# A 640-slot matmul chain of two transformer stacks: order of work changed in six stages

## The reference

```python
# first stack: four layers, kinds A, B, C, A
for i in range(4):
    xn = rms_norm(h, norm_gain[i])
    m = diff_attention | mla | rglru_block | diff_attention    # (xn) -> y @ w_out
    h = h + m
    g = sigmoid(rms_norm(h, ple_norm[i]) @ ple_w_gate[i])
    h = h + g * (p[i] @ ple_w_proj[i])
# second stack: an SSD layer, then a dilated attention layer
for layer in range(2):
    shift, scale, gate = split(silu(c) @ ada_w[layer] + ada_b[layer], 3)
    hh = x * (1.0 + scale) + shift
    y = ssd_mixer(hh) | dilated_mixer(hh, k_sh, v_sh)
    x = layer_norm(alpha * x + (1.0 + gate) * y) * ln_g[layer] + ln_b[layer]
    if layer == 0:
        k_sh, v_sh = split(x @ kv_w, 2)
```

## Time and profile before

| | |
|---|---|
| median of 3 runs | 3638.04 us (3634.32 to 3638.28) |
| the profiled execution's own time | 3631.8 us |
| its span, first to last instruction | 3630.0 us |
| mean granted TensorE clock over the span | 0.987 |
| PE busy / DVE busy / ACT busy / POOL busy | 96% / 78% / 54% / 16% |
| mean rate of the transfers | 190 GB/s |

### The profile page before, as it was taken

One profiled execution on the slowest core, in us unless ns is written; L12 is line 12 of the kernel. 1 busy time (PEld: TensorE's weight loads), 2 busy tenths in 40 slices (PEclk: granted clock), 3 DMA queues, 4 the chain that ended last, 5 costly groups with the idle time before them and its releaser, 6 DMA issues.

```text
span 3630.0 us, 68468 instructions
## 1 busy us (share of the span) xinstructions
PE 3492.7 (96%) x27986; PEld 3410.1 (94%) x27986; DVE 2836.3 (78%) x4649; ACT 1948.7 (54%) x3084; POOL 579.3 (16%) x546
## 2 busy tenths in 40 slices
PE   7999999999999999999999999999999998999997
PEld 7999999999899989999999999999999997999997
DVE  7787887677787887877877787898989866666665
ACT  6555546566547685565555456554545546434344
POOL 2111112111113011221111112231313300000000
PEclk9999999999999999999999999999999998999998
DMA  6555556434465444656555464445454443555552
GB/s 244 211 196 216 198 222 225 172 151 175 167 274 189 175 157 182 254 180 228 198 219 202 188 251 175 152 156 216 152 209 161 154 151 123 203 204 192 208 193 93
DMA packets 104904, 691.17 MB, mean 190 GB/s; under 512 B 12688, under 2 KB 21008, under 8 KB 22672
## 3 DMA queue, kind: packets, MB, share of 16 engines
q1 hardware_dynamic: 104128, 685.14, 50.9%
q0 software_dynamic: 464, 1.64, 0.1%
HBM read 676.25 MB, written 2.10 MB: 187 GB/s over the span
## 4 chain that ended last, share of the span: by engine, by line
PE 48%; DVE 15%; ACT 5%; issue 3%; POOL 1%; DMA 1%; SPq 0%; DVEq 0%; POOLq 0%; ACTq 0%
PE g L434 14%; PE g L436 14%; PE g L435 14%; DVE w_lo L1457 4%; ACT w_hi L944 2%; DMA scratch<-scratch 1%; POOL scratch L2271 1%; PE turn_bank L473 1%; DVE scratch L1987 1%; DVE con L1987 1%; DVE sq L1951 0%; DVE scratch L1958 0%; DVE sq L1950 0%; PE norm_bank L447 0%; DVE rstd L1950 0%
## 5 line engine op out<-in xcount | busy, mean ns | idle before, releaser
L1457 DVE TENSOR_TENSOR w_lo<-w_raw,w_hi 128x1024 fp32r<-128x1024 f32 x1088 | 1342.9, 1236 | 445.7 <-ACT w_hi L944 433.5
L944 ACT ACTIVATE w_hi<-w_raw 128x1024 fp32r<-128x1024 f32 x1088 | 1134.0, 1054 | 978.1 <-PE g L436 855.2
L434 PE MATMUL g<-p_hi,w_hi 128*128 128x256 f32 x4624 | 1333.0, 288 | 35.0 <-DVE w_lo L1457 23.1
L435 PE MATMUL g<-p_lo,w_hi 128*128 128x256 f32 x4624 | 1310.9, 283 | 0.0
L436 PE MATMUL g<-p_hi,w_lo 128*128 128x256 f32 x4624 | 1310.8, 283 | 0.0
L434 PE MATMUL g<-q_hi,w_hi 128*128 128x256 f32 x3472 | 1004.5, 289 | 18.4 <-DVE scratch L2164 10.5
L436 PE MATMUL g<-q_hi,w_lo 128*128 128x256 f32 x3472 | 986.3, 284 | 0.0
L435 PE MATMUL g<-q_lo,w_hi 128*128 128x256 f32 x3472 | 986.3, 284 | 0.0
L434 PEld LDWEIGHTS g<-p_hi,w_hi 128*128 128x128 f32 x4624 | 889.4, 192 | 49.5 <-DVE w_lo L1457 33.2
L435 PEld LDWEIGHTS g<-p_lo,w_hi 128*128 128x128 f32 x4624 | 889.7, 192 | 1.4
L436 PEld LDWEIGHTS g<-p_hi,w_lo 128*128 128x128 f32 x4624 | 889.2, 192 | 0.0
(11 more groups left out here) (421 smaller groups left out, 3833.1 us busy)
## 6 DMA issues: line engine op xcount, KB each, us to landing
w_raw<-in_slots SPq DMA_DIRECT2D x640, 1024.0 KB, 4.9
scratch<-scratch SPq DMA_DIRECT2D x128, 64.0 KB, 4.9
h<-in_x SPq DMA_DIRECT2D x4, 512.0 KB, 6.3
out_h<-h SPq DMA_DIRECT2D x4, 512.0 KB, 2.6
sq<-in_p POOLq DMA_DIRECT2D x4, 256.0 KB, 3.0
con<-in_consts SPq DMA_DIRECT2D x1, 832.0 KB, 10.9
scratch<-in_distance POOLq DMA_DIRECT2D x1, 576.0 KB, 5.6
vec<-in_vecs SPq DMA_DIRECT2D x1, 383.0 KB, 3.8
```

What stands on the lines that cost most here:

```text
L434: pe.matmul(g, wh, hi[:, k], start=n == 0, stop=False)
L435: pe.matmul(g, wh, lo[:, k], start=False, stop=False)
L944: act.activation(w_hi[k % SPLIT][:, cols], raw[MAIN_AT[k] % RAW][:, cols], ACT.Copy).then_inc(hi_ready, 1)
L1457: dve.tensor_tensor(w_lo[k % SPLIT][:, cols], raw[MAIN_AT[k] % RAW][:, cols], w_hi[k % SPLIT][:, cols], SUB).then_inc(lo_ready, 1)
```

## The change

- **A heads (layers 0 and 3).** The modulation's half slots move from slots 2, 3, 6, 7 to slots 1, 2, 5, 6; the column sums from slot 1 to slot 0. The loads of these slots move with them.
- **Ends of A layers.** The projection begins with banks that the scores do not use, the modulation's column sums follow, and the first two output tiles are multiplied in parts (`begin_out`, `begin_tile`, `part`): blocks of the seven finished heads between the last head's turn, mix and norm, and its own two blocks at the end.
- **End of B and C.** In B the first output tile is multiplied in parts likewise (the last pair gives its last two blocks). In C the projection waits for the split p alone, and the first output tile takes y's blocks as they come.
- **SSD.** Rows, segments, decay and weights of the first two of a group's four pieces move from the next group's steps 0 and 1 to the own group's slots 8 and 9; the other two from steps 2, 3 to 0, 1. `s_y_out` moves from steps 2 to 5 to steps 0 to 3 and waits for the gate product of its piece; norm to 5, scale to 6, `s_y_lo` to slot 7.
- **Dilated heads.** The first head begins with q0 and q1 side by side on each arriving block of q (`two_square_tiles`), then q2, the gate, and k and v (`D_FIRST`). The p blocks are made in four portions between these slots (`D_NORM_TILES`), the odd h tiles on DVE in place of ACT. Its modulation halves stand in slots 4, 5, 8, 9, and head 0's weights 0 and 1 are turned together at its end. At the layer's end the two half tiles of the first output slot are multiplied in parts, as above.
- The gates' `model_norm` uses bank bT in place of bN.

The core of the diff:

```diff
-    heads = lambda at: [at + 8 * n + m for n in range(A_HEADS) for m in (2, 6)]
+    heads = lambda at: [at + 8 * n + m for n in range(A_HEADS) for m in (1, 5)]
...
-    return out + [454 + 10 * n + m for n in range(DIL_HEADS) for m in (0, 8)]
+    return out + [454 + 10 * n + m for n in range(DIL_HEADS) for m in (0 if n else 4, 8)]
...
+D_FIRST = (0, 1, 2, 9, 3, 4, 5, 6, 7, 8)
+D_NORM_TILES = (0, 2, 6, 11, DT)
...
+        def two_square_tiles(hi, lo):
+
+            ws = [slot(), slot()]
+            pe.wait_ge(tile_taken, c.at("tile"))
+            for n in range(SLOT):
+                if n == SLOT // 2:
+                    second_half()
+                pe.wait_ge(x_lo, c.next("x"))
+                for e, w in enumerate(ws):
+                    g = G[c.bank ^ e][:, 0:SEQ]
+                    wh, wl = w_hi[w][:, n * P:(n + 1) * P], w_lo[w][:, n * P:(n + 1) * P]
+                    pe.matmul(g, wh, hi[:, n], start=n == 0, stop=False)
+                    pe.matmul(g, wh, lo[:, n], start=False, stop=False)
+                    last = pe.matmul(g, wl, hi[:, n], start=False, stop=n == SLOT - 1)
+                    if n == SLOT // 2 - 1:
+                        last.then_inc(half_used, 1)
+                    if n == SLOT - 1:
+                        last.then_inc(tile_done, 1)
+            c.next("tile", 2)
...
+        def begin_out():
+
+            w, s = slot(), c.k["slot"]
+            return w, s, begin_tile()
+
+        def begin_tile():
+
+            c.next("tile")
+            pe.wait_ge(tile_taken, c.at("tile", -2))
+            g = G[c.bank][:, 0:SEQ]
+            c.bank ^= 1
+            return g
+
+        def part(begun, hi, lo, first, last, at=0, length=SLOT):
+
+            w, s, g = begun
+            for n in range(first, last):
+                b = at + n
+                if b == SLOT // 2:
+                    pe.wait_ge(lo_ready, 2 * s)
+                wh, wl = w_hi[w][:, b * P:(b + 1) * P], w_lo[w][:, b * P:(b + 1) * P]
+                pe.matmul(g, wh, hi[:, n], start=n == 0, stop=False)
+                pe.matmul(g, wh, lo[:, n], start=False, stop=False)
+                done = pe.matmul(g, wl, hi[:, n], start=False, stop=n == length - 1)
+                if b == SLOT // 2 - 1 and length == SLOT:
+                    done.then_inc(half_used, 1)
+            if last == length:
+                done.then_inc(tile_done, 1)
...
-                if j == 1 and prev:
+                if j == 0 and prev:
                     mod_columns([acc[:]])
...
             a_head(hi, lo, False, True)
             for n in range(1, A_HEADS):
                 a_head(hi, lo, True, False)
             pe.wait_ge(p_ready, c.next("p"))
-            w = slot()
+            w, s = slot(), c.k["slot"]
+            pe.wait_ge(factor_ready, c.at("norm"))
+            proj_half(layer, 0, w, range(4), s)
+            mod_columns([acc[:]])
+            out_0 = begin_out()
+            pe.wait_ge(x_lo, c.at("x", A_HEADS - 1))
+            part(out_0, *y, 0, 4)
             pe.wait_ge(score_read, c.at("score_read"))
-            pe.wait_ge(rot_read, c.at("rot"))
-            proj_half(0, w, range(6))
+            proj_half(layer, 0, w, range(4, 8), s)
+            part(out_0, *y, 4, 10)
             a_turn_weights()
+            part(out_0, *y, 10, 14)
             a_mix()
+            out_1 = begin_out()
+            part(out_1, *y, 0, 6)
             a_norm_out()
-            pe.wait_ge(factor_ready, c.at("norm"))
-            proj_half(0, w, (6, 7))
-            c.next("x", A_HEADS)
-            mod_columns([acc[:]])
-            out_and_gates(y, x)
+            part(out_1, *y, 6, 14)
+            pe.wait_ge(x_lo, c.next("x", A_HEADS))
+            part(out_0, *y, 14, DT)
+            part(out_1, *y, 14, DT)
+            out_and_gates(layer, y, x, 2)
...
             pe.wait_ge(p_ready, c.next("p"))
-            w = slot()
+            w, s = slot(), c.k["slot"]
+            out_0 = begin_out()
+            pe.wait_ge(x_lo, c.at("x", B_PAIRS - 1))
+            part(out_0, *y, 0, 7)
             pe.wait_ge(score_read, c.at("score_read"))
-            proj_half(0, w, range(4))
+            proj_half(layer, 0, w, range(4), s)
             b_turn_weights()
-            mod_columns([acc[:]], fresh=True)
+            mod_columns([acc[:]])
+            part(out_0, *y, 7, 10)
             b_mix()
             pe.wait_ge(turn_read, c.at("turn"))
-            proj_half(0, w, range(4, 8))
-            c.next("x", B_PAIRS)
-            out_and_gates(y, x, fresh=True)
+            pe.wait_ge(factor_ready, c.at("norm"))
+            proj_half(layer, 0, w, range(4, 8), s)
+            part(out_0, *y, 10, 14)
+            pe.wait_ge(x_lo, c.next("x", B_PAIRS))
+            part(out_0, *y, 14, DT)
+            out_and_gates(layer, y, x, 1)
...
             pe.wait_ge(p_ready, c.next("p"))
-            pe.wait_ge(x_lo, c.at("x", -2))
-            proj_half(0, slot(), range(8))
-            out_and_gates(y, x)
+            w, s = slot(), c.k["slot"]
+            proj_half(layer, 0, w, range(8), s)
+            out_and_gates(layer, y, x, 0)
...
-            if 2 <= step <= 5:
-                s_out(step - 2, turned)
             if step < 4:
-                s_rows(g, step)
-            if step == 6:
+                s_out(step, turned)
+            if step < 2:
+                s_rows(g, step + 2)
+            if step == 5:
                 s_norm()
...
-                if first and n == 3:
-                    pe.wait_ge(x_lo, c.next("x", DT))
-                square_tiles(*((p_hi, p_lo) if 3 <= n <= 8 else (q_hi, q_lo)), arriving=DT if first and n == 0 else 0)
+                kind = n if prev else D_FIRST[n]
+                if not prev and n == 0:
+                    two_square_tiles(q_hi, q_lo)
+                elif prev or n > 1:
+                    square_tiles(*((p_hi, p_lo) if 3 <= kind <= 8 else (q_hi, q_lo)), arriving=DT if not prev and kind == 3 else 0)
...
+            tile_0 = begin_out()
+            pe.wait_ge(x_lo, c.at("x", DIL_HEADS - 1))
+            part(tile_0, c_hi, c_lo, 0, 4, 0, 8)
             d_turn_weights(2)
+            part(tile_0, c_hi, c_lo, 4, 7, 0, 8)
             d_turn_values(1)
-            d_turn_values(2)
             mod_columns(d_acc)
+            w, s, _ = tile_0
+            tile_1 = w, s, begin_tile()
+            part(tile_1, c_hi, c_lo, 0, 4, 8, 8)
+            d_turn_values(2, -2)
+            part(tile_1, c_hi, c_lo, 4, 7, 8, 8)
             d_mix()
             pe.wait_ge(x_lo, c.next("x", DIL_HEADS))
-            norm_project(c_hi, c_lo, 0)
+            part(tile_0, c_hi, c_lo, 7, 8, 0, 8)
+            part(tile_1, c_hi, c_lo, 7, 8, 8, 8)
+            norm_project(c_hi, c_lo, 0, 2)
...
-                if j in (2, 3, 6, 7):
-                    ada_half([acc[:]], (j - 2) % 4)
+                if j in (1, 2, 5, 6):
+                    ada_half([acc[:]], (j - 1) % 4)
...
+            p_slot()
             a_finish(jl)
-            p_slot()
...
-            if 2 <= step <= 5:
-                s_y_out(step - 2)
             if step < 4:
-                s_segments(g, step)
-            if step == 7:
+                s_y_out(g, step)
+            if step < 2:
+                s_segments(g, step + 2)
+            if step == 6:
                 s_scale_y(g)
...
+                if n > 7:
+                    s_segments(g, n - 8)
...
-        def s_y_out(m):
+        def s_y_out(g, m):
 
             dve.wait_ge(yd_done, c.next("yd"))
+            dve.wait_ge(gluon, 10 * g + 7 + m)
...
+        def d_norm_tiles(n):
+
+            for m in range(D_NORM_TILES[n], D_NORM_TILES[n + 1]):
+                dve.wait_ge(x_hi, c.next("x"))
+                if m % 2:
+                    link(dve.tensor_scalar(h[:, m], h[:, m], V("ln_g", m), V("ln_b", m), MUL, ADD))
+                dve.tensor_tensor(p_lo[:, m], h[:, m], p_hi[:, m], SUB).then_inc(x_lo, 1)
...
+                if n in ((0, 1, 8, 9) if prev else (4, 5, 8, 9)):
                     ada_half(d_acc, n % 2)
...
```

244 lines of the change are left out of this document (137 added, 107 removed).

## The result

| | before | after |
|---|---|---|
| median | 3637.52 us (3634.32 to 3638.28, 4 runs) | 3607.58 us (3605.91 to 3611.83, 4 runs) |
| ratio after/before | | 0.9918, 95% interval 0.9905 to 0.9932 |
| span of the profiled execution | 3630.0 us | 3604.5 us |
| mean granted TensorE clock | 0.987 | 0.994 |

The change saves 25.5 us between the two profiled executions and 30 us between the medians. The forecast was 3594 us with a range of 3574 to 3620.

A forecast was written before the change was run, and what follows sets the result against it. PE, busy 96% of the span, was taken as the bound. Terms -16.7, -7.3, +15, -12, -13.5 and -6.3 sum to -40.8 us: 3591.0 for the profiled execution, forecast 3594 us after a run-spread allowance, range 3574 to 3620.

The forecast's parts named there:

- Ends of the A layers: Ends of layers 0 and 3: output-tile parts fill idle and half-clock time, saving 16.7 us (bounds 8 to 18).
- Ends of B and C: Ends of layers B and C: a tile put between and an earlier projection save 7.3 us (bounds 4 to 9).
- A heads: Heads of layers 0 and 3: moved modulation halves delay the weights' turn 1.1 us a head, costing 15 us.
- SSD: SSD layer: earlier steps remove 17.2 us of PE waits, less 5.2 of new ones, saving 12 us.
- rival (b): SSD layer: gives nothing, DVE at 96% cannot be ahead, waits move to w_lo L1457; 3606 us, chance 0.13.
- the leftover wait: SSD groups: a new PE wait of 0.75 us a group, 5.2 us in all, was allowed for.
- Start of the dilated layer: Dilated layer's first tiles: paired q tiles and later k0 save 13.5 us (bounds 10 to 15).
- the two cases, full clock and half clock: Dilated layer's paired tiles: start saves 14.5 us at best, 13 if the pair stays at half clock.
- End of the dilated layer: Dilated layer's end: two half tiles multiplied in parts fill lost time, saving 6.3 us (bounds 4 to 7).

The follow-up runs named there:

- Experiment 6: Kernel after, with six of eight modulation instructions left out in the 16 output slots of layers 0 and 3: 3605.09 us, ratio to before 0.9909.
- Experiment 4: Kernel after, with A heads' modulation halves back in slots 2, 3, 6, 7 and layer-end column sums behind the mix: 3596.45 us.
- Experiments 1 and 2: Kernel after with the third piece's inputs ahead of scale_y in SSD slot 6: 3609.42 us; kernel after with the whole SSD part undone: 3606.04 us.
- Experiments 8, 9 and 3: On Experiment 4, SSD norm, scale, y_lo later: 3590.23 us; on that, first taps on ACT: 3581.14 us; kernel after, one tap omitted in groups 1-7: 3588.66 us.
- experiment 7: Kernel after, with the dilated layer's first two tiles one after another instead of side by side: 3617.8 us, ratio to before 0.9944.

## Why the prediction was right or wrong

The direction was right, and the measured 3607.58 us lie inside the range, 13.6 us above the forecast. The saving was smaller than summed, mainly because of one term, the SSD layer's.

**Ends of the A layers: right, and a quarter given back.** The first output tiles came 7.0 and 9.4 us earlier, forecast 7.2 and 9.5. The term looked no further than these tiles: behind them stand output slots in which DVE needs 5.6 us against PE's 5.77 and is idle only 0.4 to 0.7 us ahead of every second slot. It can't finish earlier by as much as PE starts earlier. PE ends the 16 tiles earlier and waits for the last blocks of the split h: 1.5 us in layer 0 and 2.4 in layer 3. Experiment 6 shows that it is this load.

**Ends of B and C: right.** 2.8 and 4.0 us against 3.1 and 4.2.

**A heads: the mechanism right, its size too large.** 10.5 us lost where 15 was forecast. The term was 2.04 - 0.96 = 1.1 us a head; measured it is 0.75. What absorbed more is the time after the maxima: without the half in slot 7 DVE stands idle for ACT's w_hi, 1.00 us before and 2.89 in the second head after, so part of the shifted chain was caught up there; that this is what took the difference is read from one head and not tested. The turn's waits grew to 18.7 us in 13 and not to about 29 in 14. The 2.04 us delayed the scores of slot 7 too, which the prediction did not list: 5.1 us in 9 on the rotation L1768. Experiment 4 gives back 7.1 us.

**SSD: wrong, and rival (b) is what happened, at another place.** The step that failed is the leftover wait, "0.75 us a group, 5.2". It measured 12.5 + 2.9 us of waits and about 3.2 us for two stretches at half clock behind them, together no less than the 17.2 us before. The prediction had the number that decides, DVE at 96% of the group without waits, and treated it as a share of the whole group. It is two stretches: slots 0 to 7, where DVE has more to do than PE and each wait of PE is DVE's backlog, and slots 8 and 9, where it has idle time that ends with ACT's next w_hi. (In the whole layer 68.0 us of DVE's idle time end at w_hi.) Moving a step inside the full stretch changes which wait shows the backlog; only work taken out of the stretch shortens it. The change took two pieces' segments out (2.8 us) and put y_lo in (1.2 us), 1.6 us less a group. But with the segments PE's rows (L804, four matmuls, 0.72 us a piece) went to slots 8 and 9 too, where PE sets the pace: 1.4 us more a group. A group lasts as long as DVE's full stretch plus PE's two slots, so 0.2 us a group were left, less than what half clock changes from run to run. This sum is an estimate worked out from the durations; what the runs show is the total. Experiments 1 and 2 are other orders with the same load: 741.6 and 738.2 us, and most of their difference is that of their half clock (13.4 and 8.2 us). Experiments 8, 9 and 3 take 1.2, 1.6 + 1.2 and 3.2 us a group off the full stretch: 735.0, 725.1 and 719.0 us, with 13.0, 3.4 and 5.2 us of half clock in them. Rival (b) had named w_lo L1457 as the new wait; it was the turn on L2088, and PE's waits for w_lo hardly changed in the whole run (23.1 us before, 24.5 after).

The added wait for the gate product in `s_y_out` does not show: no idle time of DVE in the SSD layer ends at POOL. What the nearness of POOL's products to DVE's splits costs was not tried apart from the load.

**Start of the dilated layer: right, 14.8 against 13.5.** Of the two cases, full clock and half clock, the first came: the clock rose at 3006.9, behind the pair's first 24 matmuls, four blocks. The prediction took from the Trainium skill (TensorE: Matmul & The Clock Gate, HAM oscillation) that short groups of matmuls with idle between them run at the lower clock again and again, and concluded that the pair stays at half. The conclusion left out its own numbers: at half clock 1.28 us of work meet a block every 1.13 us, so there is no idle between the groups, and the rule did not apply. With three matmuls a block PE does stop, and the trace agrees with the rule: 0.50 as long as it stops (experiment 7). Behind the rise the pair stops for each block too, and there the trace does not agree: the clock stays at 1.00.

Part of the 14.8 is luck: five of the ten traces with the pair have one stretch more at half clock there, which costs 1.5 us, so 13.3 would have come as easily. One working does not add up: beside ACT's 12 us it puts splits of 4 x 2.1, which is 8.4 us, and then reckons with 5 to 6. The forecast of the fifth tile's end, 3047.3 less what was saved ahead of the layer (6.9), is 3040.4 all the same, and it came at 3039.2.

**End of the dilated layer: mis-sized, 3.8 against 6.3.** PE's timeline has three losses: the column sums L517 stand 0.96 us for the modulation L1635 of the last slot, behind that the clock is 0.50 from 3522.3 to 3525.7, which costs 1.5 us, and the wait for c_lo is as long as before, 1.7 us. The first two make up the missing 2.5. The stretch at half clock is in five of eleven traces with this end; the six others give 70.0 us from tile 530 to 539 in place of 71.5.

```profile
3521.30 0.61 PE L517 MATMUL g<-con,scratch 128*128 128x1 f32 x4 [0.96 <-DVE scratch L1635]
...
3522.56 0.42 PE L543 MATMUL g<-c_hi,w_lo 128*128 128x256 f32 x1
...
3529.89 0.38 PE L541 MATMUL g<-c_hi,w_hi 128*128 128x256 f32 x1 [1.68 <-DVE c_lo L2267]
```

**The sum.** -40.8 forecast, -25.5 measured. SSD +13.6, what the A layers gave back +3.9, the dilated layer's end +2.5 and its start -1.3, A heads -4.5, the others +1.1: together 15.3. Rival (b) alone gave 3606 us, and the measured median is 3607.58. That these are so near is in part luck, since the other terms' errors nearly cancel (-5.8 and +7.5 us).

## What to carry to other kernels

A helper engine's busy share over a period says little when its work comes in a full and an idle part: sum its work against the bound engine's slot by slot, and count as saved only what leaves the full part. Before reordering steps there, leave one out; the time that it returns is the price of a microsecond of that engine, and it was 0.8 to 0.9 here. Before reading a difference of 2 or 3 us between two traces, count the half-clock stretches in both. Where two engines hand over within a slot, put the step that another engine waits for ahead of the one that has slack: here the six small instructions of the softmax weights, moved ahead of half a weight split and the gate product, gave 17 us.

## What the runs showed of the hardware

- Groups of matmuls on blocks that arrive every 1.13 us: with three matmuls a block PE stopped ahead of each group for 14.5 us, and the granted clock stayed at 0.50 (for 20.5 us in all). With six, PE ran without a stop at 0.50, and the clock was at 1.00 5.2 us behind the first of them. Then PE stopped ahead of each group, and the clock stayed at 1.00.
- A wait inside otherwise full work is followed by half clock in some places and not in others. In the SSD layer after, PE waits seven times at the turn, up to 2.0 us; behind two of these waits the clock is 0.50 for 3.4 us, behind three others of the same length it is not. A stretch costs 1.5 to 1.6 us, by three stages that several traces show with and without one. What tells the cases apart was not found, and the stretches fall differently in each run: in the SSD layer with the same load there are 6.3 to 13.6 us of them, and the layer lasts 738.2 to 741.7 us.
